# Expert loop of a decoder layer: weights in long rows, split per weight row, half the down product as split products

## The reference

```python
def expert_block(args):
    xb, e = args
    gu = xb @ w_gu[e] + b_gu[e]               # 1024 -> 2 x 512
    gt, up = gu[:, :D_FF], gu[:, D_FF:]
    gt = jnp.minimum(gt, SWIGLU_LIMIT)        # 7.0
    up = jnp.clip(up, -SWIGLU_LIMIT, SWIGLU_LIMIT)
    act = gt * jax.nn.sigmoid(SWIGLU_ALPHA * gt) * (up + 1.0)   # 1.702
    return act @ w_down[e] + b_down[e]        # 512 -> 1024
```

## Time and profile before

| what | value |
|---|---|
| runs | 1100.66 us median of 3 (1099.61 to 1101.83) |
| profiled execution | span 1098.0 us from the first to the last instruction; no separate time of it is given |
| PE | busy 998.4 us (91%) |
| DVE / ACT / POOL | busy 776.6 (71%) / 480.5 (44%) / 240.0 (22%) |
| chain of waits that ends last | PE 77%, of it L1739 33%, L1782 20%; DVE 15% |
| DMA | 283.49 MB, mean 258 GB/s |

### The profile page before, as it was taken

The page is one execution under the profiler, slowest core; times in us unless marked ns, Lnnn a source line. Parts: engine busy times, 40 slices in busy tenths (PEclk is TensorE's granted clock), DMA queues, the critical chain, the costliest instruction groups (busy, mean ns, idle before and its releaser), DMA issues.

```text
span 1098.0 us, 12631 instructions
## 1 busy us (share of the span) xinstructions
PE 998.4 (91%) x4143; PEld 647.5 (59%) x4143; DVE 776.6 (71%) x1148; ACT 480.5 (44%) x731; POOL 240.0 (22%) x244
## 2 busy tenths in 40 slices
PE   2689768998999994899999999999999999999993
PEld 2566546666788754665655656566565656656551
DVE  4779988876544546877777777777777777777736
ACT  5224153343322223454554545555454555545522
POOL 1233732004200002211212212122221212212010
PEclk9699879999999997799999999999999999999996
DMA  9826243044624332699999999999999999999944
GB/s 347 269 77 228 79 154 139 15 152 169 230 77 154 136 151 74 244 321 357 361 342 368 341 361 352 346 363 340 359 346 351 361 342 358 343 357 351 329 120 161
DMA packets 120088, 283.49 MB, mean 258 GB/s; under 512 B 7100, under 2 KB 8280, under 8 KB 120056
## 3 DMA queue, kind: packets, MB, share of 16 engines
q1 hardware_dynamic: 110232, 257.93, 65.4%
q0 software_dynamic: 9824, 25.15, 8.5%
HBM read 272.62 MB, written 18.96 MB: 266 GB/s over the span
## 4 chain that ended last, share of the span: by engine, by line
PE 77%; DVE 15%; issue 2%; DMA 2%; ACT 2%; POOL 1%; POOLq 0%; DVEq 0%; SPq 0%; ACTq 0%
PE ps L1739 33%; PE ps L1782 20%; PE ps L1498 11%; DVE mix L1050 4%; DVE small L1122 2%; DVE top L1121 2%; PE ps L1676 2%; PE ps L1713 2%; PE ps L1687 2%; PE ps L1533 2%; PE ps L1720 1%; PE ps L1594 1%; PE ps L1608 1%; PE ps L1775 1%; DVE area_b L1050 1%
## 5 line engine op out<-in xcount | busy, mean ns | idle before, releaser
L1253 DVE TENSOR_TENSOR whl<-ring,whl 128x1024 fp32r<-128x1024 f32 x256 | 304.1, 1222 | 115.1 <-ACT whl L901 113.6
L1739 PE MATMUL ps<-whl,xhl 128*96 128x512 f32 x1536 | 376.4, 403 | 0.0
L1739 PEld LDWEIGHTS ps<-whl,xhl 128*96 128x96 f32 x1536 | 250.8, 163 | 105.5 <-issue 0.2
L901 ACT ACTIVATE whl<-ring 128x1024 fp32r<-128x1024 f32 x256 | 260.9, 1054 | 42.5 <-PE ps L1739 40.3
L1782 PE MATMUL ps<-ring,attn 128*96 128x512 f32 x512 | 225.1, 592 | 1.2 <-ACT attn L965 1.2
L1782 PEld LDWEIGHTS ps<-ring,attn 128*96 128x96 f32 x512 | 81.0, 163 | 120.8 <-issue 119.3
L1498 PE MATMUL ps<-h_hi,wb_hl 128*128 128x512 f32 x384 | 129.0, 410 | 4.3 <-POOL wb_hl L591 4.3
L673 POOL DMA_INDIRECT moe_rows<-mix,ius x32 | 46.8, 1464 | 315.5 <-DVE mix L1369 159.6
L965 ACT ACTIVATE attn<-ps 128x384 f32<-128x384 f32 x32 | 15.7, 491 | 175.8 <-PE ps L1775 175.8
L1498 PEld LDWEIGHTS ps<-h_hi,wb_hl 128*128 128x128 f32 x384 | 74.5, 194 | 25.8 <-issue 4.7
L1369 DVE SCALAR_TENSOR_TENSOR mix<-ps,WC,attn 96x512 f32<-96x512 f32 x64 | 45.0, 742 | 51.9 <-PE ps L1782 51.9
(11 more groups left out here) (242 smaller groups left out, 1088.2 us busy)
## 6 DMA issues: line engine op xcount, KB each, us to landing
ring<-in_w_gu_dram SPq DMA_DIRECT2D x64, 2048.0 KB, 10.1
ring<-in_w_down_dram SPq DMA_DIRECT2D x32, 2048.0 KB, 13.6
ring<-in_w_ada_dram SPq DMA_DIRECT2D x12, 2048.0 KB, 9.6
ring<-in_w_in_dram SPq DMA_DIRECT2D x6, 2048.0 KB, 7.8
ring<-in_w_out_dram SPq DMA_DIRECT2D x2, 2048.0 KB, 8.2
X<-in_x_dram SPq DMA_DIRECT2D x1, 2048.0 KB, 7.9
ring<-in_w_b_up_dram SPq DMA_DIRECT2D x1, 2048.0 KB, 14.8
moe_rows<-area_b POOLq DMA_DIRECT2D x8, 256.0 KB, 3.3
```

What stands on the lines that cost most here:

```text
L901: nc.scalar.activation(whl[:, j % NG, 0, :, :], w[:, j * GK:(j + 1) * GK, :], ACT.Copy).then_inc(hi_ok, 1)
L1253: v.tensor_tensor(whl[:, j % NG, 1, :, :], w[:, j * GK:(j + 1) * GK, :], whl[:, j % NG, 0, :, :], ALU.subtract).then_inc(lo_ok, 1)
L1739: last = mm(ps[0:slots, half, :], xhl[:, a, k, :], whl[:, j % NG, b, q, :], start=False, stop=(k == KD - 1 and a == 1))
```

## The change

- The reduction index is permuted to p * 8 + k (down: p * 4 + k). A partition's weight rows then lie behind one another in DRAM: each 2 MB load is one run of 16 KB per partition. The slots now hold rows k = 0..3 and rows k = 4..7 of both halves. The token rows get the same order where h2 is written (`by_k`, read in steps of 8 words), the router's weights too, and the activations where they are computed (`by_f`, read in steps of 4).
- A buffer of `whl` is one weight row of both halves, [128, 1024]: as large as before, eight per expert. The six matmuls of a row alternate between the two banks of PSUM.
- Two of the four rows of the down weights (KFR = 2) go through the same ring of four buffers, and two of the four turned activation blocks are split too (`ahl`, ACT copy and DVE difference). The other two rows stay plain fp32.
- The sigmoid is taken by ACT straight from the gate in PSUM and limited behind it (SIG_MAX); `gate_limit` goes, and the halved weights with it. The 1 of up + 1 is in the bias.
- The order on ACT and DVE is new.

```diff
-            gu = w_gu[0, bass.ds(e, 1), :, :].rearrange("a (k p) n -> p (a k) n", p=P)
-            dn = w_down[0, bass.ds(e, 1), :, :].rearrange("a (k p) n -> p (a k) n", p=P)
-            return gu[:, :, 0:DFF], gu[:, :, DFF:2 * DFF], dn
+            gu = w_gu[0, bass.ds(e, 1), :, :].rearrange("a (p k) n -> p (a k n)", k=KD)
+            dn = w_down[0, bass.ds(e, 1), :, :].rearrange("a (p k) n -> p (a k n)", k=KF)
+            return gu[:, 0:HK * D], gu[:, HK * D:KD * D], dn
...
+        def up_at(e, i):
+            return i if isinstance(e, int) and e == 0 else e * SEQ - KFR + i
+        def down_at(e, i):
+            if isinstance(e, int) and e == NE - 1:
+                return NE * SEQ - KFR + i
+            return e * SEQ + SEQ - KFR + KD + i
...
             def load_gate(e):
-                sp.wait_ge(lo_ok, e * 2 * GP - GP)
+                sp.wait_ge(lo_ok, up_at(e - 1, HK))
...
-                sp.wait_ge(lo_ok, e * 2 * GP)
+                sp.wait_ge(lo_ok, up_at(e - 1, KD))
...
+            def hi_part(n, buf, part):
+                if not isinstance(n, int) or n >= NG:
+                    act.wait_ge(granule_used, n - NG + 1)
+                nc.scalar.activation(whl[:, buf, 0, :], part, ACT.Copy).then_inc(hi_ok, 1)
...
-            def tanh_gate(e):
-                act.wait_ge(gt_ok, e + 1)
-                nc.scalar.activation(th, gt, ACT.Tanh, scale=0.5 * ALPHA).then_inc(th_ok, 1)
+            def gate_sigmoid(e):
+                act.wait_ge(granule_used, up_at(e, KD))
+                nc.scalar.activation(th, ps[0:slots, 0, :], ACT.Sigmoid, scale=ALPHA).then_inc(th_ok, 1)
...
+                nc.scalar.activation(actT[:, KFR:KF, :], turned(6)[:, KFR:KF, :], ACT.Copy).then_inc(actT_ok, 1)
+                nc.scalar.activation(ahl[:, 0, :, :], turned(6)[:, 0:KFR, :], ACT.Copy).then_inc(ah_ok, 1)
...
+            expert(NE - 1, 1, NE // 2 - 1, last=True)
+            down_high_parts(NE - 1, 1, NE // 2 - 1)
...
+            def lo_part(n, buf, part):
+                dve.wait_ge(hi_ok, n + 1)
+                v.tensor_tensor(whl[:, buf, 1, :], part, whl[:, buf, 0, :], ALU.subtract).then_inc(lo_ok, 1)
...
-                link(v.scalar_tensor_tensor(out=h2[:, ch, :], in0=X[:, ch, :], scalar=rstd3[:, ch:ch + 1],
-                                            in1=A2b, op0=ALU.mult, op1=ALU.mult))
-                v.tensor_tensor(h2[:, ch, :], h2[:, ch, :], sh2b, ALU.add).then_inc(h2_ok, 1)
+                rows_ = h2[:, ch, :].rearrange("p (k q) -> p k q", k=KD)
+                link(v.scalar_tensor_tensor(out=rows_, in0=by_k(X[:, ch, :]), scalar=rstd3[:, ch:ch + 1],
+                                            in1=by_k(A2b), op0=ALU.mult, op1=ALU.mult))
+                v.tensor_tensor(rows_, rows_, by_k(sh2b), ALU.add).then_inc(h2_ok, 1)
...
+            def activate(up_done, th_done, gate, prod, done, n):
+                dve.wait_ge(*up_done)
+                v.tensor_scalar(up1, ps[0:slots, 1, :], LIMIT + 1.0, 1.0 - LIMIT, ALU.min, ALU.max).then_inc(gate, 1)
+                dve.wait_ge(gate, n)
+                dve.wait_ge(*th_done)
+                v.scalar_tensor_tensor(out=up1, in0=th, scalar=SIG_MAX, in1=up1, op0=ALU.min,
+                                       op1=ALU.mult).then_inc(prod, 1)
+                dve.wait_ge(prod, n)
+                v.scalar_tensor_tensor(out=av.rearrange("s (k q) -> s k q", k=KF), in0=by_f(ps[0:slots, 0, :]),
+                                       scalar=LIMIT, in1=by_f(up1), op0=ALU.min, op1=ALU.mult).then_inc(done, 1)
...
+            def expert(e, b, reused=True, last=False):
+                up_low_parts(e, b, HK, KD)
+                down_low_parts(e - 1, 1 - b)
+                if not last:
+                    up_low_parts(e + 1, 1 - b, 0, 2)
+                gated(e)
+                if not last:
+                    rows_low(e + 1)
+                    up_low_parts(e + 1, 1 - b, 2, HK)
+                weighted(e - 1, 1 - b, reused)
+                act_low(e)
...
+            def down_parts(e, parity, half_e):
+                pe.wait_ge(actT_ok, e + 1)
+                pe.wait_ge(al_ok, e + 1)
+                for i in range(KFR):
+                    pe.wait_ge(lo_ok, down_at(e, i) + 1)
+                    at = down_buffer(e, parity, i)
+                    for a, b in ((0, 0), (0, 1), (1, 0)):
+                        for half in range(2):
+                            last = mm(ps[0:slots, 2 + half, :], ahl[:, a, i, :], whl[:, at, b, half * CH:(half + 1) * CH],
+                                      start=(i == 0 and a + b == 0), stop=False)
+                    last.then_inc(granule_used, 1)
+                came(pe, SD[parity], half_e)
+                for k in range(KFR, KF):
+                    for half in range(2):
+                        last = mm(ps[0:slots, 2 + half, :], actT[:, k, :], down_w[parity][:, k, half * CH:(half + 1) * CH],
+                                  start=False, stop=(k == KF - 1))
+                last.then_inc(dn_done, 1)
```

More of the change, by code:

```diff
@@ L14 @@
+import math
 from contextlib import ExitStack
@@ L892, in _, with up_high_parts, down_high_parts @@
                 block_high(block_no["ga", m] + 2)
[L893 to L902, removed]
+            def hi_part(n, buf, part):
+                if not isinstance(n, int) or n >= NG:
+                    act.wait_ge(granule_used, n - NG + 1)
+                nc.scalar.activation(whl[:, buf, 0, :], part, ACT.Copy).then_inc(hi_ok, 1)
+            def up_high_parts(e, parity, lo, hi):
+                for i in range(lo, hi):
+                    if i % HK == 0:
+                        came(act, SU if i else SG, e)
+                    hi_part(up_at(e, i), up_buffer(e, parity, i), gu_part(i))
+            def down_high_parts(e, parity, half_e):
+                came(act, SD[parity], half_e)
+                for i in range(KFR):
+                    hi_part(down_at(e, i), down_buffer(e, parity, i), down_w[parity][:, i, :])
             for k in range(KD):
@@ L964, in actT_copy, with expert @@
                 act.wait_ge(ta_done, e + 1)
[L965 to L969, removed]
+                nc.scalar.activation(actT[:, KFR:KF, :], turned(6)[:, KFR:KF, :], ACT.Copy).then_inc(actT_ok, 1)
+                nc.scalar.activation(ahl[:, 0, :, :], turned(6)[:, 0:KFR, :], ACT.Copy).then_inc(ah_ok, 1)
+            def expert(e, b, half_e, last=False):
+                up_high_parts(e, b, HK, KD)
+                down_high_parts(e - 1, 1 - b, half_e + b - 1)
                 if not last:
-                    weights_high(e + 1, 0)
+                    up_high_parts(e + 1, 1 - b, 0, 2)
+                gate_sigmoid(e)
+                if not last:
                     rows_high(e + 1)
+                    up_high_parts(e + 1, 1 - b, 2, HK)
                 actT_copy(e)
@@ L1302, in token_softmax @@
                     last = v.tensor_scalar(wts[:, ch, :], wts[:, ch, :], sm[:, 1, ch:ch + 1], None, ALU.mult)
-                link(last)
-                v.tensor_scalar(wth[:, :, :], wts[:, :, :], 0.5, None, ALU.mult).then_inc(wt_ok, 1)
+                last.then_inc(wt_ok, 1)
             b_ = job("rank")
@@ L1409, in _ @@
+            gated(0)
+            rows_low(1)
+            up_low_parts(1, 1, 2, HK)
+            act_low(0)
+            expert(1, 1, reused=False)
+            expert(2, 0, reused=False)
+            with dve.Fori(1, NE // 2 - 1) as i:
+                expert(i * 2 + 1, 1)
+                expert(i * 2 + 2, 0)
+            expert(NE - 1, 1, last=True)
+            down_low_parts(NE - 1, 1)
             weighted(NE - 1, 1)
@@ L1789, in expert @@
                     pe.wait_ge(xl_ok, e + 1)
-                    for half in range(2):
-                        up_half_parts(e, half)
+                    up_parts(e, b, 0, KD)
                 if not last:
@@ L1834, in _ @@
                         pe.wait_ge(ov_w, n * 48 + 48)
-                        for half, w in enumerate((gate_w, up_w)):
-                            up_half(e, half, w, ov_gu)
+                        up_whole(e, ov_gu)
                         pe.wait_ge(ov_av, n + 1)
```

185 lines of the change are left out of this document (80 added, 105 removed).

## The result

The change makes the kernel slower, by a little under 2% and clear of the noise: 1120.74 us (median of 4 runs, 1120.01 to 1121.39) against 1100.13 for the kernel before on the same chip, a ratio of 1.018 [1.017, 1.020]. 1081.8 was forecast, with 1076 to 1098 as its range.

A forecast was written before the change was run, and what follows sets the result against it. PE alone was taken to bound the expert loop. Saving 21.5 us, less 2.4 (tail) and 0.4 (strided pair), plus 0.2 (scaling dropped), gave 18.9: span 1098.0 to 1079.1, plus 2.7 around it, 1081.8 us; range 1076 to 1098.

The forecast's parts named there:

- the SyncE paragraph: Load requests in the expert loop: first four rows 0.8 us late, inside a margin; last four with 2.3 us margin.
- rival A: In the loop, transfers become the bound in part: about 19.05 us per expert, 1094 us in all; chance 17%.
- Why the loads have room: Transfers in the loop: 15.4 us of loads plus 2.9 of software queue, 18.3 us per expert, under 19.35.
- Rival B: Weight loads: 16 KB rows are slower; at 350 GB/s 20.9 us per expert, about 1150 us; at 375, 1114; chance 9%.
- PE: Expert loop: splitting four of eight down products saves 0.67 us per expert, leaving 18.67; 21.5 us over 32 experts.
- Rival D: Up product: alternating banks make matmuls cost 0.238 us, losing 0.48 of 0.67 per expert; 1097 us; chance 4%.
- DVE and ACT: Expert loop: DVE 16.4 us and ACT 12.5 of 18.67 per expert, neither the longer engine; tight margins 2.1 and 1.0.
- Rival C: In the loop, DVE or ACT take over before row k = 4; strided activation at three times its length, 1097 us; 6%.
- Strided reads: Activation and h2 row operations: nearly free, 0.1 us on the activation, 0.4 on the last chunk's pair; ends 0 and 2.5.
- Tail: After the loop: the last expert's down parts are split only after its activations are copied, 3.6 us against 1.18; cost 2.4.
- other end: Last down product: PE's clock falls in the longer gap; half speed over its 6.2 us costs 6 us more.
- the start: Before the first activation: one more low part, about 2 us, offset by weights waiting ready; 0, ends -2 and +2.

The follow-up runs named there:

- the half loads: Changed kernel with each of the two gate/up slots loaded in two 1 MB requests, each sent when its two rows' low parts are made: 1089.44 us, ratio 0.989.
- the one execution of 1090.8 us: One run of the half loads plus the tail repair, with all rows in index order and nothing strided; that series measured 1081.51 us, ratio 0.982.
- long down rows: The half loads plus the tail repair, gate/up in index order, down rows in 16 KB runs with the strided activation: 1082.66 us, ratio 0.984.
- the tail repair: The half loads with the last expert's split down rows made before its activation; first run also with down rows in index order: 1085.45 us, ratio 0.986.

## Why the prediction was wrong

**The step that failed** is in the SyncE paragraph: "The last four are requested at about 9 and used 12.4 us later: margin 2.3". The 12.4 was nearly right: in the expert shown ACT is free for row 4 at 746.6, 12.9 us after the request at 733.73 (12.5 and 12.7 in two experts without the scatter). The landing was not. I set 10.1 us against it, the median of the earlier trace rows, which was made by requests 4 to 8 us apart. The change moves two requests together and a third 9 us behind them. The third then shares the engines with what is left of their 4.2 MB (the down rows asked for at 724.92 land at 743.5), and lands after 14.5 us in this expert and 14.0 in the median of the loop (12.5 to 15.7). The margin in this expert is -1.6, and ACT's wait of 1.68 us in the timeline above is that. The pattern of requests does it here together with the scatter: with the same rules and no scatter these loads land after 11.5 us, inside the margin. The text said that the first rows are requested "only once the queue has run dry", and gave this no price.

**The ring behind it** the prediction did not see. It had no late rows beyond a margin, and let the bytes decide if anything did (rival A: 19.05 us, 1094). But here a late load makes its own slot's next request late, and meanwhile DMA engines stand idle, so that bytes which fit at 18.71 us (the half loads show it) don't fit in time. Rival A named the right resource, and was neither bytes nor a sum over them: it was slower than before by 20 us, where A had 6 faster.

**"Why the loads have room"**: the sum of 18.3 us was usable, since at 18.71 us PE never waits once requests are early, with a DMA share of 0.97. A sum of bytes can't tell whether they are asked for in time.

**Rival B, long rows**, was wrong in sign: 431 GB/s, at the upper of my two ends. The Trainium skill (DMA: Bandwidth & Descriptors, Latency and other measured facts) has a large row pitch slowing copies; at this pitch of 32 KiB no run shows it, and the 3% that the prediction took over from a pitch of 512 KiB did not come.

**PE**: 18.71 where 18.67 was forecast, from the chain of the half loads: 12 split down matmuls 2.77 (2.76 forecast), the plain ones 3.43 (3.44), 48 up matmuls 11.08 (2 x 5.52). Rival D, the banks, falls with it.

**DVE and ACT**: right. Without scatter, or with half loads, no PE wait names them. Rival C falls, although its premise half came true. The timeline of the kernel after:

```profile
387.40 2.07 DVE L1308 SCALAR_TENSOR_TENSOR area_a<-X,col,attn 128x1024 f32<-128x1024 f32 x1
389.51 2.00 DVE L1310 TENSOR_TENSOR area_a<-area_a,attn 128x1024 f32<-128x1024 f32 x1
...
760.43 1.08 DVE L1389 SCALAR_TENSOR_TENSOR attn<-ps,mix 96x512 f32<-96x512 f32 x1
```

**Strided reads**: mis-sized. The activation in steps of 4 words took 1.08 us where the contiguous one has 0.69 (+0.39, not +0.1), inside its margin. The h2 pair in steps of 8 took 2.07 and 2.00 where it had 1.28 and 1.23 (the second is the earlier trace rows): 1.56 a chunk, where I put 0.4 on the last chunk alone. Four chunks make 6.2, of which some 4 show in the first copy. ACT's first copy comes at 464.9 to 467.4 in the eight kernels with the stride, and at 461.1 to 461.8 in four without it (of the other two, 463.1 with long down rows, and 468.2 in the one execution of 1090.8 us: in that one a load issued at 233.8 us in its twin goes out at 240.8 already, long before the strided rows, and why stays open). The row of 24 elements in steps of 3 misled me. The Trainium skill (Advanced Engine Details and Errata, Memory Cachelines) had it right that such an access pays; it gives no size, and the doubling in the prediction was my own bound. The prediction set it aside.

**Tail**: near in size, in another division. The chain of waits of the kernel after, behind ACT's last copy at 1082.40, and the window of the first split matmuls:

```profile
1082.95 0.95 ACT whl L920
1083.93 1.24 DVE whl L1288
1085.16 0.14 issue
1085.30 4.27 PE ps L1844 x12
1089.56 3.45 PE ps L1850 x8
```

```profile
1085.30:1087.00 1.70, 1.70 (x4) 1.19 (x5) 0.99 (x1) 1.04 (x2) 1.17 (x1) 0.50 0.00 0
```

PE starts 2.90 us after the copy's start (1.18 in the earlier trace rows, 3.6 forecast). Then its granted clock is 0.50, the lower of its two levels (1.2 GHz), and the 12 split matmuls take 4.27 us where they take 2.77 in the loop. PE had stood idle for 2.94 us; before, after 1.21 us, and with the tail repair, after 1.63, the clock stayed at 1.00. So the prediction's "other end" came in part, 1.5 us of its 6. Gap and product together take 10.6 us against 8.3: 2.3 more, where the forecast, 2.4 less the 0.67 saved in this product too, had 1.7. The gap was shorter than forecast and the product longer; that the total is as near as it is was partly luck.

**The sum redone.** By stretch of the profiled execution, against the kernel before: the forecast had +0.2 us ahead of the first copy, -20.8 in the 31 intervals and +1.7 behind the last copy, -18.9 in all. The half loads, with requests in time, have +6.1, -20.1 and +3.1, -10.9 in all. The kernel after has +4.4, +14.8 and +2.5. So the forecast's loop was right to 0.7 us with requests in time, and 34.9 us of the 35.6 that the loop missed by come and go with the requests; the start was missed by 4 to 6 us and the tail by about 1.

**What stays open.** That the DMA share is about 0.55 while a load is still under way means that some engines are done with it and others are not. In the run without the scatter the share falls from near 1 to nearly nothing within about a microsecond (0.01 in 750 to 751 us), which makes the scatter's packets the likely cause of the spread, but which engines lag was not seen, and it is not shown. Nor is it shown how the 14.0 us of landing divide between the pattern of requests and the scatter, or how much slack per expert would have been enough: no run changed PE's pace and nothing else.

## What to carry to other kernels

A load's landing time belongs to the pattern of requests it was measured in: when a change shortens the consumer or moves a request, queue every load of one period again by hand (when it is asked for, what stands ahead of it, when it is needed), and ask whether its lateness delays its own next request. Where a ring buffer's slots are given back in one piece, give them back in halves: it costs one more request per slot, and both slots so took 31 us off this kernel. And a layout that lengthens the rows of a load is not free where it puts a stride into the vector work beside it.

## What the runs showed of the hardware that I had not expected

- Loads with 16 KB runs moved 431 GB/s, against 419 and 414 with 4 KB and 406 with 2 KB, though their rows lie 32 KB apart.
- An fp32 operation of 1024 columns that reads two operands in steps of 8 words took 2.07 us against 1.28; one of 512 in steps of 4 took 1.08 against 0.69. Both are about 1.6 times as long.
- Taking the accumulating scatter away (with the gather and the rest of the software queue 8.5% of the time) brought gate/up landings from 11.4 to 8.0 us in the changed kernel and from 10.1 to 8.3 in the one before. What it delays is far more than the time that its own packets take.
- After 2.94 us without a matmul PE's granted clock was 0.50 (1.2 GHz) over the next 1.7 us, and 12 split matmuls took 4.27 us instead of 2.77; after 1.21 and 1.63 us it stood at 1.00.
- A pace of 19.38 us per expert, with two rows less through the ring, had no waits in the loop; at 18.71 us with them, the same request rules lost 1.2 us per expert on average.
